# One query-weight block kept over two chunks, the others through one buffer in two halves

## What is computed

```python
for i in range(2):
    h = rms_norm(x, norm_mix[i])
    x = x + (s5_mixer if i == 0 else dilated_attention_mixer)(h, ...)
    h = rms_norm(x, norm_ffn[i])
    x = x + peer_ffn(h, w_q[i], sub_keys[i], u_tab[i], v_tab[i])
out = rms_norm(x, norm_final)

def peer_ffn(h, w_q, sub_keys, u_tab, v_tab):        # shortened
    q = h @ w_q                                      # 1024 -> 8 heads x 2 x 128
    s = scores of q against 128 keys per half        # top 16 of each half,
    idx, gate = top 16 of the 256 sums, softmax      # then top 16 of their sums
    act = einsum('cd,ckd->ck', h, u_tab[idx])        # 128 experts per token
    return einsum('ck,ckd->cd', gate * gelu(act), v_tab[idx])
```

## Time and profile before

| | us |
|---|---|
| median of 3 runs | 1713.1 |
| lowest and highest | 1706.93 and 1715.06 |
| the profiled execution | 1716.83 |
| its span in the trace | 1715.0 |

### The profile page before, as it was taken

How to read it: one execution, slowest core, us unless ns; L and a number is a source line. 1 busy time by engine, 2 the same in 40 slices (tenths; PEclk the granted TensorE clock), 3 DMA queues, 4 the chain that set the end, 5 groups by cost and what they waited for, 6 DMA issues and landing times.

```text
span 1715.0 us, 19604 instructions
## 1 busy us (share of the span) xinstructions
PE 1287.7 (75%) x6664; PEld 551.6 (32%) x6664; DVE 1096.8 (64%) x2618; ACT 616.3 (36%) x2072; POOL 603.0 (35%) x563
## 2 busy tenths in 40 slices
PE   7995666577969868997878796799787677645555
PEld 5581221122713324333345232443252233101000
DVE  8767899644668666436547976663474848676544
ACT  7344343323243245114333332532263523234222
POOL 3223344333232244223323223332333344544441
PEclk7998787798979989997989898999898788877786
DMA  8379799999999999999999999999999999999996
GB/s 329 112 325 421 304 422 421 421 423 423 424 408 410 422 422 420 427 424 420 420 417 402 391 421 424 414 393 425 423 391 424 421 388 414 422 414 414 420 421 287
DMA packets 85925, 682.80 MB, mean 398 GB/s; under 512 B 9792, under 2 KB 10176, under 8 KB 11584
## 3 DMA queue, kind: packets, MB, share of 16 engines
q0 software_dynamic: 73728, 536.90, 75.8%
q1 hardware_dynamic: 12096, 144.64, 20.2%
HBM read 680.46 MB, written 1.05 MB: 397 GB/s over the span
## 4 chain that ended last, share of the span: by engine, by line
DMA 37%; PE 32%; DVE 15%; ACT 5%; issue 4%; POOL 3%; ACTq 0%; DVEq 0%; POOLq 0%
DMA ringmem<-experts,lay 29%; PE ps L512 11%; PE ps L577 11%; DMA wt<-w_qkv 8%; DVE ringmem L1556 7%; PE ps L592 4%; POOL ringmem L1527 3%; ACT S L1060 2%; ACT lay L1163 1%; PE ps L906 1%; PE ps L952 1%; DMA wt<-w_glu 1%; PE ps L525 1%; PE ps L763 1%; DVE area L2021 1%
## 5 line engine op out<-in xcount | busy, mean ns | idle before, releaser
L1527 POOL DMA_INDIRECT ringmem<-experts,lay x512 | 576.5, 1126 | 1042.1 <-PE ps L512 913.7
L512 PE MATMUL ps<-ringmem,S 128*32 128x512 f32 x2048 | 611.9, 741 | 367.0 <-ACT S L1060 357.9
L1556 DVE CUSTOM_DVE_ANT_0 ringmem<-ringmem,Hrep 128x1024 f32<-128x1024 f32 x384 | 463.3, 1225 | 259.2 <-DMA ringmem<-experts,lay 249.5
L512 PEld LDWEIGHTS ps<-ringmem,S 128*32 128x32 f32 x2048 | 110.8, 123 | 756.1 <-ACT S L1060 509.8
L577 PE MATMUL ps<-wt,hT 128*128 128x512 f32 x576 | 259.1, 603 | 18.3 <-DMA wt<-w_qkv 18.2
L1055 ACT ACTIVATE gelus<-dots 128x2 f32<-128x2 f32 x224 | 45.2, 202 | 602.9 <-DVE dots L1556 595.1
L1556 DVE CUSTOM_DVE_ANT_0 ringmem<-ringmem,area 128x1024 f32<-128x1024 f32 x128 | 155.8, 1225 | 124.3 <-DMA ringmem<-experts,lay 124.0
L577 PEld LDWEIGHTS ps<-wt,hT 128*128 128x128 f32 x576 | 107.5, 192 | 169.9 <-issue 159.6
L1042 ACT ACTIVATE S<-con,lay 128x32 f32<-128x32 f32 x512 | 134.6, 311 | 40.7 <-PE ps L512 40.0
L1060 ACT ACTIVATE S<-S,gelus 128x32 f32<-128x32 f32 x512 | 136.9, 314 | 24.6 <-ACT gelus L1055 1.1
L592 PEld LDWEIGHTS ps<-hT,wt 128*128 128x128 f32 x896 | 102.4, 193 | 14.0 <-issue 13.1
(11 more groups left out here) (277 smaller groups left out, 1199.4 us busy)
## 6 DMA issues: line engine op xcount, KB each, us to landing
wt<-w_qkv SPq DMA_DIRECT2D x36, 2048.0 KB
wt<-w_q SPq DMA_DIRECT2D x14, 2048.0 KB
wt<-w_glu SPq DMA_DIRECT2D x5, 2048.0 KB, 14.6
ringmem<-experts,lay POOLq DMA_INDIRECT x512
wt<-w_o SPq DMA_DIRECT2D x4, 2048.0 KB
ringmem<-w_glu SPq DMA_DIRECT2D x3, 2048.0 KB, 23.2
ringmem<-w_q SPq DMA_DIRECT2D x2, 2048.0 KB, 14.2
keysT<-keys SPq DMA_DIRECT2D x2, 1024.0 KB, 23.5
```

Of the source, the lines that this page charges most:

```text
L512: last = pe.matmul(ps[TG * t:TG * (t + 1), half, :], S[:, u % 2, i, :], ring[:, (2 * u + i) % RING, D + half * 512:D + (half + 1) * 512], ...
L1527: pool.indirect_dma_start(ring[:, s % RING, :], None, experts[phase // NC], bass.IndirectOffsetOnAxis(ap=rows[:, phase % NC, j, n:n + 1], ...
L1556: last = v.tensor_tensor_reduce(ring[:, i, 0:D], ring[:, i, 0:D], hrep(phase, j), 1.0, 0.0, ALU.mult, ALU.add, dots[:, b, second:second + 1])
```

## The change

One block of each layer stays in its slot from the first chunk to the second: `KEPT` holds item 6 (the first query block of layer 0, which is the same weights as item 0, in slot 0) and item 57 (the last query block of layer 1, the same as item 33, in slot 1). These two are not loaded any more. While a kept block occupies its slot, the other blocks (2 to 5, 7 to 9, and 34 to 56) pass the remaining slot. Each is loaded as two halves of four k-tiles, by two DMAs of 1 MB. The first half of a block is asked for when PE has done k-tile 3 of the block before it (new semaphore `half_used`), the second half when PE has done all of that block (`w_used`). PE waits for each half by its own semaphore (`half_in`), in front of k-tile 0 and of k-tile 4. The first of these blocks in each layer has its own condition for both halves. Item 2, loaded before by itself early in phase 0, is now issued with the others of its group. Blocks 10 to 33 use both slots as before. Where a block is projected in two parts, its first half is released only by the last part.

```diff
+WT1 = WT0 + ITEMS0
+KEPT = WT0 + WQ0, WT1 + 2 * ITEMS1 - 1
+KH = KT // 2
...
+def by_halves(n):
+    return n not in KEPT and (WT0 <= n < WT1 or n >= WT1 + ITEMS1)
+def halves_ahead(n):
+    return n - WT0 - (n > KEPT[0]) if n < WT1 else WT1 - WT0 - 1 + n - WT1 - ITEMS1
+def block_slot(n):
+    return (1 if n < WT1 else 0) if by_halves(n) else n % 2
+def whole_ahead(n):
+    return 0 if n < WT0 else (n - WT1) // 2 + 1
...
+                    if n in KEPT:
+                        continue
+                    if by_halves(n):
+                        u = halves_ahead(n)
+                        for half in range(2):
+                            if n in (WT0, WT1 + ITEMS1):
+                                sp.wait_ge(w_used, n - (n > WT0))
+                            elif half == 0:
+                                sp.wait_ge(half_used, u)
+                            else:
+                                sp.wait_ge(w_used, n - (n - 1 in KEPT))
+                            cols = slice(KH * BLOCK * half, KH * BLOCK * (half + 1))
+                            sp.dma_start(
+                                wt[:, block_slot(n), KH * half:KH * (half + 1)].rearrange("p k n -> p (k n)"),
+                                src[:, cols]).then_inc(half_in[half], 16)
+                        continue
...
-            weights(0, 1, 0, 1)
             next_gain(norm_event(0, 1, 0), 2)
             sp.wait_ge(idx_ready, event(0, QUARTERS - 1))
-            weights(0, 1, 1, 8)
+            weights(0, 1, 0, 8)
...
+            def arrived(n, k):
+                if by_halves(n) and k % KH == 0:
+                    pe.wait_ge(half_in[k // KH], 16 * (halves_ahead(n) + 1))
+                elif k == 0 and n not in KEPT:
+                    pe.wait_ge(w_in[n % 2], 16 * (whole_ahead(n) + 1))
...
             def project(n, bank, act):
-                pe.wait_ge(w_in[n % 2], 16 * (n // 2 + 1))
                 for k in range(KT):
-                    last = pe.matmul(ps[:, bank, :], act[:, k, :], wt[:, n % 2, k, :], start=(k == 0),
+                    arrived(n, k)
+                    last = pe.matmul(ps[:, bank, :], act[:, k, :], wt[:, block_slot(n), k, :], start=(k == 0),
                                      stop=(k == KT - 1))
+                    if by_halves(n) and k == KH - 1:
+                        last.then_inc(half_used, 1)
                 last.then_inc(w_used, 1)
...
+                    if n is not None and by_halves(n) and k == KH - 1 and ends and done is None:
+                        last.then_inc(half_used, 1)
```

More of the change, by code:

```diff
@@ L90, in item @@
         return i - WQ0 if c == 0 else WT0 + i
-    return WT0 + ITEMS0 + ITEMS1 * c + i
+    return WT1 + ITEMS1 * c + i
+def by_halves(n):
[6 more added lines that the diff above has]
+    return 0 if n < WT0 else (n - WT1) // 2 + 1
 def norm_event(layer, c, ffn):
@@ L270, in build @@
         wq_used = sem("wq_used")
+        half_in = [sem(f"half_in{h}") for h in range(2)]
+        half_used = sem("half_used")
         w_used = sem("w_used")
@@ L582, in project_turned @@
                                opens=True, ends=True):
-                if w is None:
-                    pe.wait_ge(w_in[n % 2], 16 * (n // 2 + 1))
-                    w = wt[:, n % 2]
                 for k in range(KT):
+                    if n is not None:
+                        arrived(n, k)
+                        w = wt[:, block_slot(n)]
                     if k == KT // 2 and second_half is not None:
```

## The result

The changed kernel takes 1764.34 us (median, 1759.52 to 1772.71) against 1712.96 us (1706.93 to 1716.07) on the same chip: ratio 1.0285, 95% interval [1.0259, 1.0311], 51 us slower. The forecast was 1713 with a range of 1703 to 1727. The profiled execution has a span of 1765.4 us, the one of before 1715.0, and the 50.4 us between them are what the trace has to account for. Lines of helpers have moved: L512 is now L552, L577 (`project`) L624, L581's matmuls L641, L1060 L1111.

What follows compares the result with a forecast made beforehand. The prediction took DMA to bound most of the kernel, with compute setting the pace where bytes are saved and PE also near its limit in QKV. Terms 0 - 2.0 + 0 + 2.0 = 0 gave 1713 us, own range 1708 to 1719, with rivals 1703 to 1727.

Steps and rivals of the forecast that it cites:

- Traffic: Two weight loads of 2.097 MB dropped, total 678.6 MB: 0 us in layer 0, -2.0 in layer 1, 0 last phase.
- the first rival: The saved bytes count in full, 2 x 4.97 = 9.9 us less, giving 1703 us; chance 0.14.
- the zero of layer 0: Dropping item 2's early load in layer 0 changes the time by 0 us, bounds 0 and -5.0.
- The -2.0: Layer 1, end of phase 1: without item 35's load the residual add comes 2.0 us earlier, bounds 0 and -5.0.
- Landing of a half: A half block's load takes 5.0 us of bytes plus 1.6 fixed, 6.6 us, bounds 5.8 to 11.6.
- Period, 10.0 to 10.5 us: Second chunk's QKV stages: one projection per 10.3 us instead of 9.60 and 9.48, making the last 7.0 and 8.0 late.
- "1.4 us" of the last projection: In each stage's last projection the second half of the block comes 1.4 us late once more.
- What gives the lateness back: PE's idle time behind each stage (9.4, 8.2, 13.4, 9.9, 9.3 us) exceeds the lateness before it (5.3, 4.0, 7.0, 8.0, 2.7).
- The term "+2.0": DMA time lost outright in the two QKV halves, 1 us each, bounds 0 and +15.0.
- The second: Rival: one buffer starves PE, gathers run dry in the QKV stages, 15.0 us of lateness kept, 1726 us; chance 0.20.
- The third: Rival: 8 KB rows cut the weights' DMA share from a half to a third, 1731 us; chance 0.07.
- Semaphore steps, 0: Added semaphore steps, one in mid-projection and one per half, cost 0 us, from between 0 and 23 x 0.1.

Runs made afterwards that it cites:

- e4: The kernel before, both buffers and whole blocks, with items 2 and 35 not loaded: 1718.83 us, ratio 0.9995 to the kernel before.
- e2: The changed kernel with each block loaded in four quarters of 512 KB instead of halves, one buffer: 1750.42 us, ratio 1.0166 to the kernel before.
- e10: The kernel before plus 15 lone loads of 2048 to 256 KB in phase 3, beside gathers: 1756.69 us, ratio 1.0179 to the kernel before.
- e1: The changed kernel with each block behind a kept one loaded whole by one 2 MB DMA, one buffer: 1882.36 us, ratio 1.0933 to the kernel before.
- e6: The change in layer 1 only (item 57 kept, items 34 to 56 in halves), layer 0 as before: 1753.86 us, ratio 1.0196 to the kernel before.
- e3: The kernel before, two buffers, nothing kept, each block loaded as two 1 MB DMAs waited for together: 1728.70 us, ratio 1.0050 to the kernel before.
- e8: The kernel before, two buffers, nothing kept, blocks asked for, waited for and released in halves: 1716.97 us, ratio 1.0000 to the kernel before.
- e12: The kernel before plus loads asked for several at once beside gathers, and lone loads at the end without gathers: 1796.1 us, ratio 1.0438 to the kernel before.
- e9: The kernel before with half a block kept in chunk 1 of layer 1, other halves through three half slots: 1721.56 us, ratio 1.0004 to the kernel before.

## Why the prediction was wrong

*Traffic.* Right as far as it can be told: bytes 678.60 MB, and e4 shows that the dropped loads are worth less than the 10 us of the first rival. Against the zero of layer 0 nothing speaks: the first GLU projection started at 362.72 in the changed kernel against 366.24, but at 368.28 in e2, which drops the same load, and at 367.88 in e10, which drops none. The -2.0 stays open. In e1, e2, e4 and e6, which drop the load, the boundary (last query block of phase 1 to the first QKV block) takes 45.3 to 45.7 us against 46.6 before; but in e3 and e8, which load everything, it takes 45.7 and 45.6, and in e10 and e12, which are the kernel before up to there, 50.8 and 49.9. So the 49.8 of the changed kernel, with PE at its lower clock there, can't be put down to the change. What a byte is worth is a matter of place: e10 shows 31 us for 13.4 MB in the gather-only stage.

*Landing of a half, 6.6 us: mis-sized.* "10.0 us of that and 1.6 us are fixed" split 11.6 us wrongly. By e10 and e12 it is 4.2 us plus, by the fitted rule, 7.5 for a block and 5.0 for a half: a half lands in 9.1 us under full gathers, since halving saves only its own 2.5 us of bytes. In the changed kernel the first one of the stage, asked for at 980.41 under full gathers, took 9.5 us, and the later ones in the chain 6.3 to 8.4, at 369 GB/s instead of 422; the mean of the eight first halves was 7.3. That thinner gathers shorten them fits these figures and the rule, but was not tested by itself. The bounds that I gave, 5.8 to 11.6, hold it. The Trainium skill's 2.0 us of fixed cost ("DMA: Bandwidth & Descriptors", "Anatomy of one DMA") is given there for DMAs that GpSimd issues. The loads here come from SP, and at the end, with no gathers, 256 to 2048 KB took 2.0 to 2.7 us more than their bytes at 0.42 MB per us, so it agrees roughly; beside gathers it is no guide, with 4.2 us and the turns. The rule of the Trainium skill on two transfers that the prediction cites ("DMA: Bandwidth & Descriptors", "Rules for kernel authors") speaks of disjoint partition halves, while the halves here are halves of columns over all 128 partitions; for these e3 measured a loss of 0.5%.

*Period, 10.0 to 10.5 us: wrong, and this is the step that failed.* The series "asked for 3.55 us into the projection" plus the landing was there, and with 6.6 it gave 10.2. Measured were a hold of 4.6 us in the mean, 3.7 at the full clock and 5.4 where it had fallen, and a landing of 7.3; with the 0.14 us from landing to the first matmul that is 12.0. Since PE's own work takes 9.5 us, all beyond it is loss, so an error of 1.7 in the period tripled the loss per block, from 0.70 and 0.82 us to 2.37 and 2.56. The QKV halves became late by 8 x 2.37 = 19.0 and 8 x 2.56 = 20.5 us, not 7.0 and 8.0; GLU and the query blocks of layer 0 likewise. (The "1.4 us" of the last projection was a slip too: 15.15 - 13.85 is 1.3.)

*What gives the lateness back: right at the period forecast, wrong at the period that came.* e3 and e9 had first periods of 10.6 and 10.3 us, about as forecast here, and gave back all but 1 us of their 7.7 and 5.9 us. In the changed kernel the account fails. "Each is more than the lateness before it" compared PE's idle time with PE's lateness. But that idle time is a wait for gathers, and the gathers were late too. A ring buffer comes free when PE has done its slot; when PE runs slow, POOL asks later (9.2 us for PE in one wait instead of 6.9), and the DMA has less to do: 369 GB/s against the 422 possible is 96 x 53 / 422 = 12.1 us lost, and 363 is 97 x 59 / 422 = 13.6 us. Lost DMA time wasn't given back in this kernel, which needs the DMA right after: of 19.0 and 20.5 us, 4.4 and 7.2 came back (start to start in the table). The term "+2.0" for both halves should have been 14.6 + 13.3 = 27.9. My upper bound, 15.0, was the lateness kept whole, but taken from the too short period.

*Sum by the prediction's terms.* 9.3 (layer 0) + 3.1 (to the end of phase 1) + 3.2 (the boundary) + 14.6 + 13.3 + 5.1 + 5.9 - 4.1 (the last phase) = 50.4. The terms 3.1, 3.2, 5.9 and -4.1 lie in or at the edge of what the same stretches differ by among runs that have no single buffer in them. So 42.3 of the 50.4 us are placed; whether the other 8.1 belong to the change stays open.

*Rivals.* The second, "one buffer starves PE and it stays so", is what happened: it was to decide above 9.9 us "with the DMA share clearly under 1.00", and both came (12.0, 0.96), at nearly twice its price of 15.0. A period above 9.9 us alone doesn't do it: e3 had 10.6 at a share of 0.99. The third had a mechanism of the kind that fits e10 and e12, turns, at wrong shares: I dismissed it because "10 of 11.6 us" looked like a half share, but that figure was my own split of one number. The first falls by e4: 1703 would be a ratio of 0.994, under its interval of [0.9966, 1.0023].

*Semaphore steps, 0:* e8 shows no cost, to within 0.3%.

## What to carry to other kernels

Before giving up a buffer, take hold time plus landing time over the number of buffers and compare it with the consumer's own period; here (7.1 + 11.6) / 2 = 9.4 was just under 9.5, and 4.6 + 7.3 = 11.9 for one half slot was far over. It is a floor: e2's quarters give 2.0 + 8.2 = 10.2 and took 11.5 and 10.5, and e9's three half slots should have run at PE's own 9.5 and took 10.3 and 9.8. Splitting a transfer shortens the hold, but beside the full gathers here half the size still took 9.1 of 12.0 us to land, so it doesn't replace a buffer; an additional part slot does (e9). And when an engine that frees buffers for the bounding stream runs late, count the stream's lost time as lost if a stage that needs it in full follows, and ask of saved bytes in which stage they are saved.

## What the runs showed of the hardware

- A load of 256 KB beside gathers takes 7.25 us, one of 2048 KB 12.0; alone 2.65 and 7.7. Most of a small load's landing is other traffic.
- The share of DMA busy time falls less than the bytes do when the queues run thin: 1.00 at 415 GB/s, 0.96 at 363 to 369, 0.90 at 320 in the changed kernel from 1020 to 1030, and 0.68 at 263 in e1's first QKV half. Read GB/s.
- Behind waits of 2.06 and 2.73 us a projection took 8.80 us instead of 7.1, its first four k-tiles 5.38 instead of 3.69, and the granted clock of that stage was 0.93 instead of 1.00: part of it ran at the lower level, 1.2 GHz. Behind waits of 2.42 and 2.90 us in the second half it took 7.11, so the length of the wait alone doesn't tell.
- With the same bytes in the same slots, two DMAs instead of one (e3) cost 0.5%: one more turn per block, 2.5 us by the fitted rule, gives (7.1 + 14.2) / 2 = 10.65 us as an estimate, and 10.56 and 10.05 were measured in the two QKV halves.
